# Order of the extra expert pairs, and filler products in TensorE's waits, in a two-layer hybrid diffusion step

## What is computed

```python
def _hier_moe(h, w_group, w_expert, w_gate, w_up, w_down):
    # top-1 group of 4, then top-2 experts of the 8 in it
    ...
    hid = jax.nn.silu(jnp.einsum('td,edf->tef', t, w_gate)) * jnp.einsum('td,edf->tef', t, w_up)
    out = jnp.einsum('tef,efd->td', hid * combine.astype(h.dtype)[:, :, None], w_down)
...
x = _layer_norm(ALPHA * x + m[5] * _hier_moe(_modulate(x, m[3], m[4]), *moe), ln_g[l, 1], ln_b[l, 1])
```

## Time and profile before

| | us |
|---|---|
| median of 3 runs | 1292.52 |
| lowest and highest | 1288.12, 1296.45 |
| profiled execution | 1289.75 |
| its span, first to last instruction | 1287.9 |
| TensorE busy | 1188.9 (92%) |
| VectorE / ScalarE / GpSimd busy | 597.9 / 352.0 / 186.9 |
| mean granted TensorE clock | 0.978 of full speed |

### The profile page before, as it was taken

How to read it: one execution, slowest core, us unless ns; L and a number is a source line. 1 busy time by engine, 2 the same in 40 slices (tenths; PEclk the granted TensorE clock), 3 DMA queues, 4 the chain that set the end, 5 groups by cost and what they waited for, 6 DMA issues and landing times.

```text
span 1287.9 us, 17510 instructions
## 1 busy us (share of the span) xinstructions
PE 1188.9 (92%) x6755; PEld 680.1 (53%) x6755; DVE 597.9 (46%) x1173; ACT 352.0 (27%) x695; POOL 186.9 (15%) x177
## 2 busy tenths in 40 slices
PE   5999999999999989999999877999999998999774
PEld 2554555545546577456555435755555555555441
DVE  2223333310136666768432217079986865332218
ACT  1333444421214543212122125311023111221122
POOL 1000000010000001131323120800000332222210
PEclk9999999999999999998999898999999998999988
DMA  9504476773211204826799969021114438999973
GB/s 348 210 25 177 142 254 239 289 270 114 89 33 40 74 10 163 340 83 232 299 407 409 406 244 393 23 91 66 66 66 171 156 128 316 392 410 408 354 293 150
DMA packets 99666, 269.79 MB, mean 209 GB/s; under 512 B 12811, under 2 KB 15154, under 8 KB 98690
## 3 DMA queue, kind: packets, MB, share of 16 engines
q1 hardware_dynamic: 83632, 234.55, 48.3%
q0 software_dynamic: 15632, 34.02, 7.1%
q10 hardware_dynamic: 322, 0.12, 0.0%
HBM read 257.68 MB, written 31.93 MB: 225 GB/s over the span
## 4 chain that ended last, share of the span: by engine, by line
PE 78%; DVE 6%; DMA 6%; SPq 4%; ACT 3%; issue 2%; ACTq 0%; POOLq 0%; DVEq 0%
PE ps L2285 18%; PE ps L2296 14%; PE ps L2797 8%; PE ps L2814 4%; PE ps L2175 4%; PE ps L2437 3%; DMA ln_rows<-in_moe_w_up 3%; PE ps L2600 3%; PE ps L2785 2%; PE ps L2581 2%; PE ps L2404 2%; PE ps L2746 2%; SPq L710 1%; PE ps L2699 1%; SPq L707 1%
## 5 line engine op out<-in xcount | busy, mean ns | idle before, releaser
L2285 PE MATMUL ps<-h_cm,weights 128*128 128x512 f32 (+1 forms) x832 | 226.8, 434 | 0.0
L2285 PEld LDWEIGHTS ps<-h_cm,weights 128*128 128x128 f32 x832 | 126.3, 191 | 104.0 <-issue 103.7
L2296 PE MATMUL ps<-weights,mix_cm 128*128 128x512 f32 x256 | 112.2, 595 | 0.0
L1769 DVE SCALAR_TENSOR_TENSOR scratch<-scratch,taps_cm 128x655 f32<-128x655 f32 x120 | 101.5, 897 | 2.5 <-ACT scratch L1325 1.0
L2296 PEld LDWEIGHTS ps<-weights,mix_cm 128*128 128x128 f32 x256 | 47.9, 190 | 56.5 <-issue 56.4
L2067 DVE TENSOR_TENSOR scratch<-ps,scratch 128x128 f32<-128x128 f32 x38 | 11.1, 292 | 143.1 <-ACT scratch L1373 143.1
L2296 PE MATMUL ps<-weights,h_cm 128*128 128x512 f32 (+1 forms) x208 | 71.4, 502 | 0.0
L2797 PE MATMUL ps<-weights,scratch 128*64 128x256 f32 x384 | 68.3, 389 | 1.8 <-DMA weights<-in_moe_w_up 1.8
L1442 DVE COPY mod_parts<-ps 128x512 f32<-128x512 f32 x24 | 16.6, 691 | 93.3 <-PE ps L2175 93.3
L1697 DVE SCALAR_TENSOR_TENSOR mix_cm<-mix_cm,gate_rows,ps 128x128 f32<-128x128 f32 x152 | 46.0, 345 | 25.1 <-PE ps L2545 23.0
L2296 PEld LDWEIGHTS ps<-weights,h_cm 128*128 128x128 f32 x208 | 36.3, 190 | 35.6 <-issue 35.6
(11 more groups left out here) (449 smaller groups left out, 2133.1 us busy)
## 6 DMA issues: line engine op xcount, KB each, us to landing
weights<-in_mod_w SPq DMA_DIRECT2D x13, 2048.0 KB, 8.9
x_tm<-in_mod_w SPq DMA_DIRECT2D x10, 2048.0 KB, 8.6
weights<-in_moe_w_gate SPq DMA_DIRECT2D x24, 512.0 KB, 11.6
weights<-in_moe_w_up SPq DMA_DIRECT2D x24, 512.0 KB, 13.4
weights<-in_moe_w_down SPq DMA_DIRECT2D x24, 512.0 KB, 15.7
scratch<-in_moe_w_down SPq DMA_DIRECT2D x21, 512.0 KB, 12.9
weights<-in_ab_w_in SPq DMA_DIRECT2D x5, 2048.0 KB, 12.8
weights<-in_cd_w_in SPq DMA_DIRECT2D x5, 2048.0 KB, 16.0
```

The costliest lines, as they stand in the source:

```text
L1769: ins = V.scalar_tensor_tensor(out=CO[:, j, 0:655], in0=UP[:, j, k:k + 655], scalar=CW[:, 4 * k + j:4 * k + j + 1], in1=CO[:, j, 0:655], o ...
L2285: ins = T.matmul(ps(*name)[:, a:b], w[:, k, col:col + 128], HT[:, k, a:b], start=(k == 0), stop=(k == KD - 1))
L2296: ins = T.matmul(ps(*name)[:, at:at + w.shape[2]], src[:, k, t * 128:t * 128 + 128], w[:, k, :], start=(k == 0), stop=(k == KD - 1))
```

## The change

Extra pairs: TensorE now works off x1's gate and up ahead of x0's down, ScalarE and VectorE drain the results one pair later (the order of the main pairs), and SyncE loads the gates and ups of both pairs ahead of the downs of both, each behind its own value of `x_slot`. The four expert numbers are read ahead of the first load.

Products on constants: a new helper `keep_busy(at, count)` multiplies the identity by constants into a PSUM place that is overwritten before anything reads it. It is called ahead of six waits: 4 products of 512 columns before the first experts' rows in layer 1; 1 and 3 before the turns of tiles 0 and 1 behind layer 0; 1 before the router product of tile 4 in each layer; and in the main pairs 5 products of 256 columns before pair 14 of layer 0 and 4 before pair 13 of layer 1.

```diff
@@ SyncE, loop over quads
-                        for p in range(2):
-                            pair = [sp.value_load(EXI[0:1, bass.ds(j * 4 + (2 * p + i), 1)], min_val=0, max_val=NE - 1) for i in range(2)]
-                            for part in range(2):
-                                sp.wait_ge(m["x_slot"], j * 4 + (1, 3, 3, 4)[2 * p + part])
+                        four = [sp.value_load(EXI[0:1, bass.ds(j * 4 + i, 1)], min_val=0, max_val=NE - 1) for i in range(4)]
+                        for part in range(2):
+                            for p in range(2):
+                                sp.wait_ge(m["x_slot"], j * 4 + (1 + 2 * part + p))
                                 for i in range(2):
-                                    load_expert(l, pair[i], FIRST_EXTRA + 2 * p + i, m[f"xw{p}"], m[f"xwd{p}"], (part,))
+                                    load_expert(l, four[2 * p + i], FIRST_EXTRA + 2 * p + i, m[f"xw{p}"], m[f"xwd{p}"], (part,))
@@ ScalarE, pairs
-                        if u >= behind:
-                            first_half(n0, s0, u - behind, frees)
-                    if behind:
-                        first_half(n0, s0, count - 1, frees)
+                        if u:
+                            first_half(n0, s0, u - 1, frees)
+                    first_half(n0, s0, count - 1, frees)
@@ VectorE, pairs: the order that main pairs had now holds for the extra ones too
-                        if not behind:
-                            if u + 1 < count:
-                                turned(n0, u + 1)
-                            second_half(n0, s0, u)
@@ TensorE
+            def keep_busy(at, count):
+                for _ in range(count):
+                    T.matmul(at, ident, C[:, 0:at.shape[1]], start=True, stop=True)
             def mixed_sum(l, t):
+                open_group(pe, "ys", l, t)
+                if l and t == 0:
+                    keep_busy(ps("ys", l, t)[:, 0:512], 4)
                 pe.wait_ge(d_y[t], 32 * (l + 1))
-                open_group(pe, "ys", l, t)
@@ x_turn1
+                open_group(pe, "xT", 1, t)
+                keep_busy(ps("xT", 1, t)[:, 0:512], (1, 3, 0, 0, 0)[t])
                 pe.wait_ge(ln_normed, NT + t + 1)
-                open_group(pe, "xT", 1, t)
@@ router_product
+                    open_group(pe, "lg", l, t)
+                    if t == 4:
+                        keep_busy(ps("lg", l, t)[:, 0:512], 1)
                     emptied(pe, "hT", l, t)
-                    open_group(pe, "lg", l, t)
@@ main pairs
+                    if (l, u) in ((0, 14), (1, 13)):
+                        pe.wait_ge(m["hc"], u - 1)
+                        keep_busy(pair_bank(u)[:, 0:256], 5 - l)
@@ extra pairs
+                        def extra_down(u):
+                            pe.wait_ge(m[f"xwd{u}"], j * 32 + 32)
+                            down(n0, u, FIRST_EXTRA + 2 * u)
                         for u in range(2):
                             pe.wait_ge(m[f"xw{u}"], j * 64 + 64)
                             gate_up(n0, u, FIRST_EXTRA + 2 * u)
                             if u == 0:
                                 extra_turn(1)
+                            else:
+                                extra_down(0)
                             turn_hidden(n0, u)
-                            pe.wait_ge(m[f"xwd{u}"], j * 32 + 32)
-                            down(n0, u, FIRST_EXTRA + 2 * u)
+                        extra_down(1)
```

More of the change, by code:

```diff
@@ L1363, in first_half, with pairs @@
                     A_(ZT[:, u % 2, 0:512], result_bank(u, 0), ACT.Copy).then_inc(m["ya"], 1)
-                def pairs(n0, s0, count, frees, behind):
+                def pairs(n0, s0, count, frees):
                     turned(n0, 0)
@@ L1375, in pairs @@
                             turned(n0, u + 1)
-                        if u >= behind:
-                            first_half(n0, s0, u - behind, frees)
-                    if behind:
-                        first_half(n0, s0, count - 1, frees)
+                        if u:
+                            first_half(n0, s0, u - 1, frees)
+                    first_half(n0, s0, count - 1, frees)
                 emptied(act, "tb", l)
-                pairs(0, 0, NP0, (FIRST_EXTRA // 2, FIRST_EXTRA // 2 + 1), 1)
+                pairs(0, 0, NP0, (FIRST_EXTRA // 2, FIRST_EXTRA // 2 + 1))
                 act.wait_ge(rt_ready, l + 1)
@@ L1386, in _ @@
                     with act.Fori(0, quads) as j:
-                        pairs(j * 2 + NP0, j * 16 + 8 * NP0, 2, (0, 1), 0)
+                        pairs(j * 2 + NP0, j * 16 + 8 * NP0, 2, (0, 1))
                 def broadcast(kind, dst):
@@ L2059, in second_half, with pairs @@
                     V.tensor_copy(ZT[:, u % 2, 512:1024], result_bank(u, 1)).then_inc(m["yv"], 1)
-                def pairs(n0, s0, count, behind):
+                def pairs(n0, s0, count):
                     turned(n0, 0)
@@ L2067, in pairs @@
                         V.tensor_tensor(HID[:, u % 2, :], pair_bank(u)[:, 128:256], SG[:, u % 2, :], ALU.mult).then_inc(m["hid"], 1)
-                        if behind:
-                            if u + 1 < count:
-                                turned(n0, u + 1)
-                            if u:
-                                second_half(n0, s0, u - 1)
+                        if u + 1 < count:
+                            turned(n0, u + 1)
+                        if u:
+                            second_half(n0, s0, u - 1)
                         dve.wait_ge(m["ht"], n0 + (u + 1))
@@ L2076, in pairs @@
                         V.tensor_copy(HIDT[:, u % 2, :], pair_bank(u)[:, 256:384]).then_inc(m["hc"], 1)
-                        if not behind:
-                            if u + 1 < count:
-                                turned(n0, u + 1)
-                            second_half(n0, s0, u)
-                        if behind and u == 4:
+                        if u == 4:
                             weights_of_pairs()
-                    if behind:
-                        second_half(n0, s0, count - 1)
+                    second_half(n0, s0, count - 1)
                 extra_blocks()
-                pairs(0, 0, NP0, 1)
+                pairs(0, 0, NP0)
                 dve.wait_ge(rt_ready, l + 1)
@@ L2091, in _ @@
                     with dve.Fori(0, quads) as j:
-                        pairs(j * 2 + NP0, j * 16 + 8 * NP0, 2, 0)
+                        pairs(j * 2 + NP0, j * 16 + 8 * NP0, 2)
                 if l == 0:
```

## The result

| | us |
|---|---|
| before, median of 9 | 1292.94 |
| after, median of 9 (1294.44 to 1298.65) | 1296.72 |
| ratio | 1.0028, 95% interval 1.0015 to 1.0042 |
| profiled execution after, its span | 1295.46, 1293.7 (before: 1289.75, 1287.9) |

The forecast was 1291.5. The change costs 3.8 us, and the profiled executions stand 5.8 us apart in span. The time stays inside the range, but the sign is wrong: a gain was forecast and a loss clear of the interval came.

The account below looks back on a forecast made before the run. The prediction took the chain of waits through x1's weight DMAs and the last scatter's issue as the bound. Terms -0.1 + 0.3 - 0.8 - 0.4 = -1.0 us took 1292.5 to 1291.5; range 1286 to 1297.5.

Parts of the forecast that it names:

- The router, tile 4: One product ahead of tile 4's router product fits its wait: nothing in layer 0, -0.4 us in layer 1.
- Products outlast the wait at the end: Rival: at 1.2 GHz throughout, layer 1's four end products delay the sum, +1.7 us, so 1294; chance 0.12.
- my term: Four products ahead of layer 1's experts' rows raise the clock earlier for the sum: -0.8 us.
- The extra pairs: New pair order: weights earlier, against GpSimd's longer chain and a late gather: -0.1 us layer 0, +0.3 layer 1.
- the 2.6 that I had named as a sign: Sign in the profile after: x1's gate/up starts 2.6 to 3.8 us earlier relative to x0's.
- GpSimd's chain: Behind x0's scatter, gather and column copy take 4.2 us before GpSimd can look at x1's result.
- The rival by which weights don't come earlier: Rival: x1's gates and ups land less than 2.7 us earlier; +4 to +6 us, 1297; chance 0.13.
- Layer 0: Extra pairs in layer 0: x1's gate/up 2.8 us earlier, its scatter 2.7 later relative to that: -0.1 us.
- The size of layer 1: Extra pairs in layer 1: x3's turn waits 1.5 us for its gather, last scatter at 1244.5 against 1244.22: +0.3 us.
- Pairs 14 and 13, turns behind layer 0: Products there gain nothing: the next weight wait takes pair 14's 2 us; the turns' reader on ScalarE starts no earlier.

Follow-up runs that it names:

- experiment 1: The change without the one product ahead of tile 4's router product in each layer: 1293.86 us, ratio 1.0014 to the kernel before.
- experiment 2: The kernel before with only the one product ahead of tile 4's router product added in both layers: 1295.12 us, ratio 1.0024.
- experiment 3: The change with keep_clock(0) behind the router at 7 products instead of 3: 1293.25 us, ratio 0.9999 to the kernel before.
- experiment 11: The kernel before with the product ahead of tile 4's router product and keep_clock(0) at 7 products instead of 3: 1289.91 us, ratio 0.9987.
- experiment 7: The kernel before with only the four products ahead of the experts' rows in layer 1 added: 1293.60 us, ratio 1.0013.
- experiment 5: Experiment 3 with GpSimd's loop body reordered, both gathers, then both index columns, then both scatters: 1291.43 us, ratio 0.9992 to the kernel before.
- experiment 9: Experiment 5 without the four products at layer 1's end: 1289.40 us, ratio 0.9981 to the kernel before.
- experiment 4: The kernel before with the new order of the extra pairs on all engines and none of the change's products on constants: 1293.19 us, ratio 1.0002.
- experiment 6: Experiment 4 with GpSimd's loop body reordered, both gathers, then both index columns, then both scatters: 1290.86 us, ratio 0.9986 to the kernel before.
- experiment 12: Experiment 9 without the products ahead of pairs 14 and 13 and of the turns behind layer 0: 1289.75 us, ratio 0.9991 to the kernel before.
- experiment 10: The change without the four products at layer 1's end: 1296.14 us, ratio 1.004 to the kernel before.
- experiment 8: Experiment 5 with layer 1's four end products placed one ahead of each of two norm broadcasts and two behind: 1295.85 us, ratio 1.0031 to the kernel before.

## Why the prediction failed

**The router, tile 4 (taken 0 in layer 0 and -0.4 us in layer 1; the runs: +3.0).** This is the step that failed. I asked who reads the product's result, and found VectorE with 0.62 us of waiting. I didn't follow what stands behind the product on TensorE's own queue, `keep_clock(0)` and the wait for the mask. I had counted the low clock only as a loss. There it was also what filled a wait, and with it kept the next slow stretch away from `keep_clock(1)`, which delays `tb`. Experiments 1, 2 and 3 show it by removal, alone and by filling. The term itself was right for what it looked at: with the cover (experiments 3 and 11) the routers' stretch is 0.6 us shorter, all of it in layer 1. The cost on TensorE's own queue, which I put at nothing, is 2.8 to 3.0 us a layer in the trace of after.

**Products outlast the wait at the end (a rival, 0.12; my term was -0.8).** No run shows my gain. By the medians the products cost 2.1 us in experiment 7, 2.0 in experiment 5 against 9, and 0.6 in the change. The first and the last are within the noise, and their traces show 0.2 and 0.1 us. Only in experiment 5 did the rival happen: nearly the whole of the four at 1.2 GHz, and 2.7 us lost in the traces. What I missed: they take 5.2 to 6.6 us where the clock is low at their start, and the wait is 3.5.

**The extra pairs (taken +0.2 together; experiment 4: +0.3 by the ratio, with an interval from -1.4 to +1.9, and +1.1 by the medians).** This part came out by its own steps. Against `tb`, x1's gate and up came 3.3 us earlier in layer 1 and 2.7 in layer 0 (taken 2.8); against x0's it was 2.9 and 2.2, so in layer 0 less than the 2.6 that I had named as a sign. GpSimd's chain is 4.35 us long (4.2), and x3's turn waits 1.74 us for its gather (1.5). The rival by which weights don't come earlier is refuted. Layer 0 came out at 0.0 against -0.1. The size of layer 1 was off, +1.7 against +0.3, since the clock fell in x3's gate and up (5.23 against 3.67 us). I had named that for x1 alone. Experiments 5 and 6 (-1.8 and -2.3 us) show that GpSimd's order cost something in the new pair order. That the new pair order is worth anything with it is not shown: no interval of the order with gathers first, but without the router's two edits, lies below 1 (experiment 6), and beside experiment 11 nothing is left of it.

**Pairs 14 and 13, turns behind layer 0 (taken 0).** Experiment 12 agrees. Pair 14's gate and up starts behind a wait of 1.74 us at full clock, and TensorE then waits 1.96 us for pair 15's weights, as said.

**The sum.** Taken out of the change, the router's product is worth 2.4 us by the means (experiment 1), and filling its wait 3.4 (experiment 3), the order +0.3 to +1.1 (experiment 4) and the end nothing (experiment 10). That makes 2.7 to 4.5, and the change measures +3.8 to +4.6 against the medians of before. In the traces the two routers lose 5.25 us. How the rest of that is absorbed on the way isn't shown. The parts aren't independent, since each moves the clock of the next: in experiments 3 and 5 it is x1's gate and up of layer 0 that takes 5.4 us instead of 3.7.

**Where luck came in.** 1296.72 lies next to the 1297 of "the weights don't come earlier", but that rival's mechanism isn't in the trace, and the cause that is there was in no rival. The range held because it took in that rival and half of the runs' spread. The spread was also a poor measure of what can be told: I had named 1% (12.9 us), and nine runs of each kernel gave the ratio to 0.14%.

## What to carry to other kernels

Before speeding up a stretch that ends in a wait on its own engine, look at that wait: time saved there turns into idle time, and on TensorE idle time can come back as a slow stretch behind it. A product on constants has two ends to check: whether it ends inside its wait at the low clock as well, and which wait the products behind it no longer cover once they run faster. When work is reordered on one engine, write out the queues of the others in the new order; here a gather that had been free came to stand between two scatters.

## What the runs showed of the hardware

TensorE's granted clock fell while the engine was 100% busy. Before, it was at 0.50 right behind 5.5 us of broadcasts on one partition; in after it fell within them, 7.25 us at a mean of 0.74. In experiment 5 it fell within them too (7.56 us at 0.71), and stayed low through full products: 6.50 us, 100% busy, at 0.54. In experiment 8 two full products, each alone between broadcasts, didn't bring it back (7.72 us at 0.50). That the broadcasts are the cause isn't shown, since no run leaves them out. The Trainium skill ("TensorE: Matmul & The Clock Gate", Part 1) says that busy-ness releases the throttle; here busy-ness alone doesn't, and the measurement decides.

A gather that GpSimd issued among saturated weight loads (DMA share 1.03) was there 7.08 us later. The last quad's gather of experiment 10, with the DMA engines nearly idle (DMA share 0.10), took 2.1 us.
